# Layer norm chain inside the attention with its sums on VectorE, two output tiles in token halves, padded keys, feed forward ends in PSUM

## The reference

```
x = x + 0.5 * swiglu(rmsnorm(x), w_gate, w_up, w_down)          # ffn1
u = rmsnorm(x) @ w_in                                           # 1024 -> 1792
y_conv = silu(layernorm(depthwise_conv31(a * sigmoid(gate)) + conv_b))      # 512 channels
y_attn = attention in a window of 128 keys on either side, 8 query heads,
         2 key heads, ALiBi bias, one sink logit per head       # 512 channels
x = x + concat(rmsnorm(y_conv), rmsnorm(y_attn)) @ w_out
x = x + 0.5 * swiglu(rmsnorm(x), ...)                           # ffn2
```

## Time and profile before

| | us |
|---|---|
| median of 3 runs | 1880.98 (1877.15 to 1881.37) |
| the profiled execution | 1878.36 |
| its span (first to last instruction) | 1876.5 |
| PE busy | 1832.3 (98%) |
| DVE busy | 957.2 (51%) |
| ACT busy | 755.4 (40%) |
| POOL busy | 1136.6 (61%) |

### The profile page before, as it was taken

The page is one execution under the profiler, slowest core; times in us unless marked ns, Lnnn a source line. Parts: engine busy times, 40 slices in busy tenths (PEclk is TensorE's granted clock), DMA queues, the critical chain, the costliest instruction groups (busy, mean ns, idle before and its releaser), DMA issues.

```text
span 1876.5 us, 24971 instructions
## 1 busy us (share of the span) xinstructions
PE 1832.3 (98%) x8120; PEld 1492.6 (80%) x8120; DVE 957.2 (51%) x1137; ACT 755.4 (40%) x988; POOL 1136.6 (61%) x595
## 2 busy tenths in 40 slices
PE   6999999999999999999999999999999999999996
PEld 5888888878678888888878888887876888888885
DVE  7644543369736454443355444334885554444334
ACT  2433332246756333332333333223576643333221
POOL 3544457769767444457744444676885854444774
PEclk8999999999999999999999999999999999999998
DMA  4322223321012323223332222333211232222331
GB/s 146 117 96 101 89 76 100 106 96 63 25 56 91 110 90 101 88 78 95 120 98 94 101 92 83 85 101 112 69 45 46 68 107 95 101 91 79 93 95 57
DMA packets 53425, 166.68 MB, mean 89 GB/s; under 512 B 6000, under 2 KB 6256, under 8 KB 53360
## 3 DMA queue, kind: packets, MB, share of 16 engines
q1 hardware_dynamic: 52128, 163.78, 27.6%
q10 hardware_dynamic: 1232, 2.10, 0.3%
HBM read 163.76 MB, written 2.10 MB: 88 GB/s over the span
## 4 chain that ended last, share of the span: by engine, by line
PE 90%; issue 4%; POOL 3%; DVE 3%; DMA 0%; DVEq 0%; POOLq 0%; ACTq 0%
PE bank L1136 29%; PE bank L1138 29%; PE bank L1137 29%; PE bank L1266 1%; DVE xs_hi L846 1%; PE bank L1279 1%; PE bank L1253 1%; DVE xs_lo L778 1%; POOL w_lo L396 1%; POOL x L517 1%; POOL diag L456 0%; POOL y_conv L447 0%; PE bank L1254 0%; PE bank L1255 0%; PE bank L1154 0%
## 5 line engine op out<-in xcount | busy, mean ns | idle before, releaser
L396 POOL TENSOR_TENSOR w_lo<-stage,w_hi 128x1024 fp32r<-128x1024 f32 x352 | 892.3, 2536 | 639.1 <-ACT w_hi L537 638.7
L537 ACT ACTIVATE w_hi<-stage 128x1024 fp32r<-128x1024 f32 x352 | 372.9, 1061 | 885.4 <-PE bank L1138 881.5
L1136 PE MATMUL bank<-xs_hi,w_hi 128*128 128x512 f32 x1688 | 663.0, 393 | 19.4 <-POOL w_lo L396 11.3
L1137 PE MATMUL bank<-xs_lo,w_hi 128*128 128x512 f32 x1688 | 658.6, 390 | 0.0
L1138 PE MATMUL bank<-xs_hi,w_lo 128*128 128x512 f32 x1688 | 658.5, 390 | 0.0
L1136 PEld LDWEIGHTS bank<-xs_hi,w_hi 128*128 128x128 f32 x1688 | 318.0, 188 | 89.8 <-issue 13.0
L1137 PEld LDWEIGHTS bank<-xs_lo,w_hi 128*128 128x128 f32 x1688 | 318.1, 188 | 66.6 <-issue 1.4
L1138 PEld LDWEIGHTS bank<-xs_hi,w_lo 128*128 128x128 f32 x1688 | 318.0, 188 | 66.7
L805 DVE TENSOR_TENSOR work<-bank,rstd 128x512 f32<-128x512 f32 x176 | 120.7, 690 | 401.0 <-PE bank L1138 400.1
L1136 PE MATMUL bank<-h_hi,w_hi 128*128 128x512 f32 x704 | 273.9, 389 | 0.0
L1137 PE MATMUL bank<-h_lo,w_hi 128*128 128x512 f32 x704 | 273.9, 389 | 0.0
(11 more groups left out here) (146 smaller groups left out, 1352.4 us busy)
## 6 DMA issues: line engine op xcount, KB each, us to landing
stage<-w_gu SPq DMA_DIRECT2D x176, 512.0 KB, 3.3
stage<-w_down SPq DMA_DIRECT2D x64, 384.0 KB, 3.1
stage<-w_down SPq DMA_DIRECT2D x64, 320.0 KB, 2.9
stage<-w_in SPq DMA_DIRECT2D x24, 512.0 KB, 3.3
stage<-w_out SPq DMA_DIRECT2D x16, 512.0 KB, 3.3
x<-xT ACTq DMA_DIRECT2D x4, 512.0 KB, 6.5
stage<-w_in SPq DMA_DIRECT2D x8, 256.0 KB, 2.7
out<-result SPq DMA_DIRECT2D x8, 256.0 KB, 2.2
```

The costliest lines, as they stand in the source:

```text
L396: nc.gpsimd.tensor_tensor(w_lo[:, r, :], stage[:, r, :], w_hi[:, r, :].bitcast(F32), ALU.subtract).then_inc(split, 1)
L537: nc.scalar.activation(w_hi[:, r, :], stage[:, r, :], ACT.Copy).then_inc(hi_made, 1)
L1136: nc.tensor.matmul(to, wh, mh, start=first, stop=False)
L1137: nc.tensor.matmul(to, wh, ml, start=False, stop=False)
```

## The change

Six edits. (1) The feed forward's sum stays in its PSUM bank: VectorE forms 0.5 * bank + x in the bank, copies it to x, and makes xs_hi, the square and xs_lo from the bank; TensorE's down tiles are written out, and tile m + 4 waits until tile m is split. The next stage's first tile waits for the fifth split before it starts. (2) k_hi and k_lo get one 128-row copy per key head with zeros in the other head's 64 rows; score matmuls use 128 rows. (3) VectorE's last 20 taps come with units 0 to 15 instead of 0 to 19. (4) The mean comes after unit 18, centring with units 19 to 22, squares with 20 to 23, their sums on VectorE with 23 to 25, the variance after unit 27, its root on ScalarE with unit 28. (5) High and low parts of the attention's result are made in two halves of 256 tokens; those of the first half with units 24 to 29. (6) The first two output tiles are computed in halves too, with the spread of the layer norm's root between them.

```diff
-LATE_TAPS = 20
+LATE_TAPS = [1] * 9 + [2, 1, 2, 1, 2, 1, 2]
...
-                add_channel_squares()
...
+                def high_k(t):
+                    scaled_ready(t)
+                    for kv in range(N_KV_HEADS):
+                        rows = slice(HEAD_DIM * kv, HEAD_DIM * (kv + 1))
+                        nc.scalar.activation(k_hi[rows, kv, :], in_bank(t)[rows, :], ACT.Copy).then_inc(qk_hi, 1)
...
-                    if 25 <= u < 29:
-                        square_channels(u - 25)
+                    if 20 <= u < 24:
+                        square_channels(u - 20)
+                    if u == 24:
+                        act.wait_ge(o_evicted, l * N_GROUPS + N_GROUPS // 2)
+                    if 24 <= u < 28:
+                        high_attention(u - 24, 0)
+                    if u == 28:
+                        root(l, "var", by_token=True)
                     if c == 0 and 3 <= g < 7:
                         mix_high(12 + g - 3)
-                root(l, "var", by_token=True)
                 evict_o(N_GROUPS - 1)
                 act.wait_ge(o_evicted, l * N_GROUPS + N_GROUPS)
                 for c in range(NC):
-                    high_attention(c)
+                    high_attention(c, 1)
...
-                with dve.Fori(0, ND // 4) as i:
-                    dve.wait_ge(par_landed, l * 16 + 16)
-                    for j in range(4):
-                        m = i * 4 + j
-
-                        tile_summed(l, base + 2 * NF + m * 4 + 3)
-                        nc.vector.scalar_tensor_tensor(chunk(x, m), bank[j][:], 0.5, chunk(x, m), ALU.mult,
-                                                       ALU.add).then_inc(evicted, 1)
-                        own(l, turns + 2 * NF + m)
-                        dve.wait_ge(sq_added, prep * ND + m)
-                        nc.vector.tensor_tensor(sq[:], chunk(x, m), chunk(x, m), ALU.mult).then_inc(squared, 1)
-                        high_x(m, par, gain_at)
-                        split_x(prep, m, par, gain_at)
+                dve.wait_ge(par_landed, l * 16 + 16)
+                for m in range(ND):
+                    new_x, no = bank[m % BANKS][:], (2 * l + h_base // NF) * ND + m + 1
+                    tile_summed(l, base + 2 * NF + m * 4 + 3)
+                    nc.vector.scalar_tensor_tensor(new_x, new_x, 0.5, x[:, m, :], ALU.mult,
+                                                   ALU.add).then_inc(x_summed, 1)
+                    dve.wait_ge(x_summed, no)
+                    nc.vector.tensor_copy(x[:, m, :], new_x).then_inc(x_kept, 1)
+                    nc.vector.tensor_scalar(xs_hi[:, m, :], new_x, par[:, gain_at + m:gain_at + m + 1], None,
+                                            ALU.mult).then_inc(x_hi_made, 1)
+                    dve.wait_ge(x_kept, no)
+                    dve.wait_ge(sq_added, prep * ND + m)
+                    nc.vector.tensor_tensor(sq[:], new_x, x[:, m, :], ALU.mult).then_inc(squared, 1)
+                    dve.wait_ge(x_hi_made, prep * ND + m + 1)
+                    nc.vector.scalar_tensor_tensor(xs_lo[:, m, :], new_x, par[:, gain_at + m:gain_at + m + 1],
+                                                   xs_hi[:, m, :].bitcast(F32), ALU.mult,
+                                                   ALU.subtract).then_inc(x_split, 1)
...
+                def add_channel_squares(c):
+
+                    dve.wait_ge(y_squared, l * 3 * NC + c + 1)
+                    if c > 1:
+                        dve.wait_ge(squares_added, l * (NC - 1) + c - 1)
+                    nc.vector.tensor_tensor(channel_squares[0], channel_squares[0], channel_squares[c],
+                                            ALU.add).then_inc(squares_added, 1)
+
+                def split_attention(c, half):
+
+                    at = slice(half * SEQ // 2, (half + 1) * SEQ // 2)
+                    dve.wait_ge(y_hi_made, l * 3 * NC + half * NC + c + 1)
+                    nc.vector.scalar_tensor_tensor(xs_lo[:, c, at], y_attn[:, c, at],
+                                                   par[:, G_ATTN + c:G_ATTN + c + 1],
+                                                   xs_hi[:, c, at].bitcast(F32), ALU.mult,
+                                                   ALU.subtract).then_inc(y_split, 1)
...
-                    if u == 24:
+                    if u == 19:
                         dve.wait_ge(stat_made, stat_no(l, "mean") + 1)
-                    if 24 <= u < 28:
-                        centre(u - 24)
+                    if 19 <= u < 23:
+                        centre(u - 19)
+                    if 23 <= u < 26:
+                        add_channel_squares(u - 22)
+                    if 26 <= u < 30:
+                        split_attention(u - 26, 0)
...
+                    split_attention(c, 1)
...
+                    if prep is not None:
+                        pe.wait_ge(x_split, prep * ND + BANKS + 1)
...
+                    if m < BANKS:
+                        open_bank(l, turns + 2 * NF + m)
+                    else:
+                        pe.wait_ge(x_split, next_prep * ND + m - BANKS + 1)
+                    f = 0
+                    for n, count in enumerate(DOWN):
+                        take(l, base + 2 * NF + m * 4 + n)
+                        pe.wait_ge(h_split, l * 2 * NF + h_base + f + count)
+                        for k in range(count):
+                            last = triple(bank[m % BANKS][:], *weights(n, k), h_hi[:, f, :], h_lo[:, f, :], f == 0,
+                                          f == NF - 1)
+                            f += 1
+                        last.then_inc(used, 1)
...
-                    nc.tensor.matmul(to, q_hi[rows, c, q], k_hi[rows, keys], start=True, stop=False)
-                    nc.tensor.matmul(to, q_hi[rows, c, q], k_lo[rows, keys], start=False, stop=False)
-                    nc.tensor.matmul(to, q_lo[rows, c, q], k_hi[rows, keys], start=False,
+                    nc.tensor.matmul(to, q_hi[:, c, q], k_hi[:, kv, keys], start=True, stop=False)
+                    nc.tensor.matmul(to, q_hi[:, c, q], k_lo[:, kv, keys], start=False, stop=False)
+                    nc.tensor.matmul(to, q_lo[:, c, q], k_hi[:, kv, keys], start=False,
...
+                def attention_tiles(between):
+
+                    take(l, MIX_S + 16)
+                    for half in range(2):
+                        at = slice(half * SEQ // 2, (half + 1) * SEQ // 2)
+                        for m in range(2):
+                            if half == 0:
+                                open_bank(l, MIX_T + OUT_A_TURN + m)
+                            for c in range(NC):
+                                if m == 0:
+                                    pe.wait_ge(y_split, l * 3 * NC + half * NC + c + 1)
+                                last = triple(in_bank(m)[:, at], *weights(16 % RING, 4 * m + c),
+                                              xs_hi[:, c, at], xs_lo[:, c, at], c == 0, c == NC - 1)
+                            if half:
+                                last.then_inc(used if m else half_used, 1)
+                        if half == 0:
+                            spread_factors(l, "var")
+                    for m in range(2, ND):
+                        if m % 2 == 0:
+                            take(l, MIX_S + 16 + m // 2)
+                        open_bank(l, MIX_T + OUT_A_TURN + m)
+                        out_tile(16, m, xs_hi, xs_lo, 0, between)
...
-                    if u == 22:
+                    if u == 18:
                         channel_mean()
-                channel_variance()
+                    if u == 27:
+                        channel_variance()
                 weigh_values(N_GROUPS - 1)
-                spread_factors(l, "var")
-
-                out_tiles(16, OUT_A_TURN, xs_hi, xs_lo, 0,
-                          {(2, 0): attention_statistic, (3, 0): lambda: spread_factors(l, "attn")})
-                out_tiles(20, OUT_C_TURN, y_hi, y_lo, NC,
-                          {(0, 1): conv_statistic, (1, 2): lambda: spread_factors(l, "conv")})
+
+                attention_tiles({(2, 0): attention_statistic, (3, 0): lambda: spread_factors(l, "attn")})
+                channel_tiles({(0, 1): conv_statistic, (1, 2): lambda: spread_factors(l, "conv")})
```

130 lines of the change are left out of this document (54 added, 76 removed).

## The result

The changed kernel takes 1865.47 us (median of 4 runs, 1863.45 to 1866.73), the kernel before, beside it, 1879.07 (4 runs). The ratio is 0.992, 95% interval 0.9907 to 0.9933: 0.8% faster, clear of the noise. The forecast was 1860.0 in a range of 1849 to 1871; as a difference of medians it was 20.98, and 13.6 was measured. The profiled execution took 1863.45 us for a span of 1861.6; against the forecast of 1857.4 for such an execution that is 14.9 saved instead of 20.95. The question is where the other 6.0 went.

What follows compares the result with a forecast made beforehand. TensorE, holding 90% of the chain of waits, was taken as the bound. 4.05 - 1.1 + 0 + 11.0 + 7.0 = 20.95 us saved from 1878.36 gives 1857.4 profiled, 1860.0 as a median; range 1849 to 1871.

Steps and rivals of the forecast that it cites:

- three feed forward ends: Feed forward ends with work following: xs_hi from PSUM no longer waits for GpSimd, TensorE's wait goes; 4.05 us saved.
- last end: Kernel's own end: the square moves behind the copy and xs_hi, so what waits for it starts later; 1.1 us lost.
- start: First tile waits for the fifth split, but as many matmuls are done by 27.62; 0, or 1.6 us lost.
- after the attention: Attention's end: early variance at full clock, shorter wait, half tiles; third output tile 5.8 us earlier, 11.0 us saved.
- padded keys: Attention units: 128-row scores avoid row changes, 0.38 us a unit; 3.5 us per layer, 7.0 us saved, ceiling 8.6 per layer.
- Rival D: After the attention: the shorter wait of 1.1 us still lets the clock fall; 1874 us, chance 0.08.
- VectorE's 15.05 of 15.60: Attention from 464.50 to 480.10: VectorE is busy nearly throughout, so padding was taken to save 0.5 us there.
- At most 2.4 can go: Attention from 480.10 to 497.40: VectorE, with four more taps, has 14.9 of 17.3 us; 1.5 us taken as saved.
- rival A: Attention: the other engines set the pace and padding brings nothing; 1867 us, chance 0.20.
- The three sums on VectorE: Before the variance: VectorE's three additions of squares fit, with 3 us spare covering 2.4 us of lateness behind one w_lo.
- the lock: VectorE and GpSimd share a port pair; VectorE instructions with two SBUF inputs contend, so the three additions may be blocked.
- Rival C: Attention: TensorE's pauses grow and the clock falls for half its work or more; 32 us slower, 1913 us, chance 0.03.

Runs made afterwards that it cites:

- run 1: Changed kernel with the score matmuls on 64 rows again: 1870.16 us, ratio 0.9941 to the kernel before.
- run 2: Changed kernel with the convolution's statistic after all twelve matmuls of the first convolution tile instead of after six: 1860.73 us, ratio 0.9891.
- run 4: Changed kernel with xs_hi at the feed forward ends made from the copy of x in SBUF instead of from the PSUM bank: 1867.09 us.
- runs 5 and 6: Changed kernel without VectorE's 20 late taps per layer, first with padded keys, then with scores on 64 rows: 1861.64 and 1867.0 us.
- run 10: Changed kernel with the later convolution statistic and the variance's three additions on GpSimd, ahead of its last w_lo: 1875.51 us.
- run 3: Kernel before with only the feed forward end edit (sum in PSUM, down tiles written out, their waits): 1877.96 us, ratio 0.9972.
- runs 8 and 9: Changed kernel, later convolution statistic; first GpSimd's tap and channel additions spread later (1865.44 us), second only its first channel addition moved to group 3 (1861.79 us).

## Why the prediction was right, and where it wasn't

The direction, the range and most mechanisms held; the forecast itself was 5.5 too low as a median, and of the gain it promised two thirds came. By its own steps, in us saved over the profiled execution:

| step | forecast | measured | from |
|---|---|---|---|
| three feed forward ends | 4.05 | 4.1 | 1.29 + 0.15 + 2.67, landmarks |
| last end | -1.1 | -0.8 | x sum 15.7 earlier, span 14.9 |
| start | 0 | -0.15 | statistic 35.19 for 35.04 |
| after the attention | 11.0 | 10.0 | 148.38 - 143.44, and 5.06 in layer 1 |
| padded keys | 7.0 | 3.5 | 1.75 + 1.79, run 1 |
| statistic behind six matmuls | not seen | -2.0 | 2 x (36.10 - 35.08) |
| sum | 20.95 | 14.65 | 14.9 between the executions |

The 0.25 between the last two numbers I can't attribute; it arises between the last feed forward's statistic and its end. The large errors all point the same way, so the range held without help from errors that cancel. The difference of the medians is 1.3 smaller than that of the two executions; run 2 shows one thing that can make it so.

**Feed forward ends: right in mechanism and size.** xs_hi was taken at 0.69 and measured 0.74; run 4 shows that the source is what matters.

**Start: right.** The first matmul is at 18.87 and the statistic 0.15 later. The reason was half wrong. The prediction read the clock as low until 27.62. The rows between those it shows say otherwise:

```profile
14.01 0.47 PE L1136 MATMUL bank<-xs_hi,w_hi 128*128 128x512 f32 x1
14.31 0.40 PE L1137 MATMUL bank<-xs_lo,w_hi 128*128 128x512 f32 x1
```

From there to the wait of 2.99 the pitch is 0.23, so the clock rose, fell in that wait and rose again; the count of 28 matmuls by 27.62 stands even so. In the changed kernel it rose after some 3.9 us of work (the pitch goes from 0.43 to 0.23 at 22.8), not after the 5.7 that the prediction carried over, but the statistic then waits 0.61 for GpSimd, the bound that it named.

**After the attention: right.** Wait 0.95 for 1.1, pitch 0.12 for 0.12, spread 0.17 after the last half matmul. Rival D did not occur: the clock held after that wait (1.00 from 519 to 530). What is missing is 0.5 a layer.

**Padded keys: the step that failed in size.** The price of a change of rows was right (0.39 for 0.38 a unit); what it is worth was not. Three things, by the table and in the prediction's stretches. Up to unit 8 it took 0.5 and got 0. It named VectorE's 15.05 of 15.60 as the limit, but with 4 us less on VectorE padding still got 0 there (runs 5 and 6). "From 480.10 to 497.40 VectorE has 12.27 of work ... At most 2.4 can go": 1.4 came, near the 1.5 taken, but for another reason. It came wholly from its second half; in the first half nothing could, because GpSimd's group is 8.02 long, full, and GpSimd never stood in that step. The row had it, 13.57 of 17.30 over two groups of which only the first is full: an average over a stretch with two limits. From unit 16 to 20 came 1.0 of the 1.5, and from unit 24 to 28 0.7 was lost that had no term. Of this 0.4 is a longer wait for ScalarE's eviction of a group (L617), 0.78 instead of 0.39; ScalarE works there without a pause. The other 0.3 lies ahead of the variance, which starts 0.68 after unit 27 instead of 0.44: VectorE's last sum of squares ends at 513.50, and where it ends earlier against unit 27 (run 4) the 0.3 is not there. Ahead of the last two sums VectorE's den for the last group had fallen behind w_lo:

```profile
508.52 2.83 POOL L399 TENSOR_TENSOR w_lo<-stage,w_hi 128x1024 fp32r<-128x1024 f32 x1
509.05 2.33 DVE L983 TENSOR_TENSOR den<-p_sum,sink_exp 128x4 f32<-128x4 f32 x1
```

It held up those sums but not ScalarE's eviction: in run 10 it takes 0.15, and the wait for the eviction is still 0.78. So the true answer lay between the forecast and rival A, and the total near A's 1867 for a different sum: A gave padding nothing and knew nothing of the statistic.

**The statistic: the step that is missing.** The prediction costed the halves and not the order of matmuls in the rewritten loop for the other tiles. Its label (0, 1) was unchanged in the diff, and only counting the matmuls ahead of it on both sides shows the move. It cost 2.0 us in the profiled execution, and 1.6 more wherever the clock falls behind it (run 2). That this statistic waited 0.40 even before was the sign that nothing ahead of it was free.

**The three sums on VectorE: right, with nothing to spare.** They ended at 513.50 for a variance at 513.56, so the 3 us of spare time were used up, and 0.3 more. The additions themselves ran at 0.7 to 0.8, but the last two stood behind den, which GpSimd blocked for over 2 us: the lock was in the prediction, its victim was another.

**Rival C** was given 0.03 with half of a layer's attention at the lower clock. Run 3 shows a fall of one group in each layer on nearly the kernel before. Its eight runs spread over 8.4 us, about two such falls, and the kernel before's eleven beside it over 6.6; which of them had falls is not shown, since one execution of each kernel was profiled. As a rival it should have been priced per group, at 4 us, and given more.

## What to carry to other kernels

Before an operation is moved or a loop rewritten, count on each engine's queue what stands ahead of every waiting instruction on both sides of the diff, also of those whose text is unchanged. When TensorE's work shrinks inside a pipeline, add up each other engine's work from one hand-over to the next, not its share of a long stretch: the engine with a group's length in work sets that group, and gains there are zero. Where VectorE and GpSimd block each other, a tiny instruction can cost as much as the long one that it lands behind, and putting work off moves it beside others; runs 8 and 9 paid that. A wait of a little over 1 us on TensorE can cost more than itself, because the clock may fall behind it.

## What the hardware showed that I had not expected

- A 128x4 addition on VectorE, 0.15 us by itself, was open for 2.33 us behind GpSimd's w_lo (run 1: 0.36, run 9: 2.00, run 10: 0.15), as long as a 128x512 xs_hi from SBUF (2.35 in run 4).
- The granted clock can fall in the middle of the attention although TensorE waits less than half a microsecond at a time and is busy 8.2 of 9.0 us (run 3, 0.50 from 473 to 482). In the profiled execution of the kernel before, with nearly the same rows, it did not; whether that is the kernel or the execution is not shown.
- Behind the same wait of 1.31 it fell in 4 of 12 layers, for some 3 us each time, and cost 1.6 (run 2).
- At the start the clock rose some 3.9 us into the work in the changed kernel (18.87 to 22.8). In the kernel before it rose 2.7 us into it (11.29 to 14.0), and after the waits of 2.99 and 1.64 only at 27.62, 5.7 us behind the last of them.
- Padding 64 rows to 128 makes a matmul of 384 columns no dearer (0.17 to 0.18 apart in both) and saves 0.39 in a unit's two changes of rows, 0.28 on the way into the scores and 0.11 on the way out.
